# Gate one-hots of a PEER layer: where the row one-hots are written and how the column one-hots are divided

## What is computed

```python
def chunk(args):
    tc, ec, gc = args
    a = jnp.einsum('td,thkd->thk', tc, u_tab[ec])
    w = (gc * jax.nn.gelu(a)).astype(tc.dtype)
    return jnp.einsum('thk,thkd->td', w, v_tab[ec])
```

## Time and profile before

| | us |
|---|---|
| median of three runs | 2521.72 (2521.64 to 2522.34) |
| span of the profiled execution | 2525.9 |
| PE busy in it | 2230.9 (88%) |
| DVE busy | 1553.5 (62%) |
| ACT busy | 1185.2 (47%) |
| POOL busy | 1123.5 (44%) |
| first gate matmul of the first layer starts at | 792.92 |
| its last group of matmuls starts at | 903.67 |

### The profile page before, as it was taken

One profiled execution on the slowest core, in us unless ns is written; L12 is line 12 of the kernel. 1 busy time (PEld: TensorE's weight loads), 2 busy tenths in 40 slices (PEclk: granted clock), 3 DMA queues, 4 the chain that ended last, 5 costly groups with the idle time before them and its releaser, 6 DMA issues.

```text
span 2525.9 us, 46629 instructions
## 1 busy us (share of the span) xinstructions
PE 2230.9 (88%) x16556; PEld 2138.3 (85%) x16556; DVE 1553.5 (62%) x2319; ACT 1185.2 (47%) x2092; POOL 1123.5 (44%) x472
## 2 busy tenths in 40 slices
PE   5797789999997589999998967999999956999998
PEld 4686679999996588989997856899999955999998
DVE  7577348993004977888885952699800088555554
ACT  8522434555545743333433232455554476444443
POOL 0002036988886545555550301588988854000000
PEclk9798789999998999999998987999999999999999
DMA  7632144555553036556553312345555500555553
GB/s 264 216 115 78 45 141 134 183 179 187 183 181 102 0 116 218 206 209 224 208 215 120 125 34 92 125 151 190 181 180 181 182 17 0 175 182 182 183 183 108
DMA packets 103456, 378.58 MB, mean 150 GB/s; under 512 B 11489, under 2 KB 11873, under 8 KB 102881
## 3 DMA queue, kind: packets, MB, share of 16 engines
q1 hardware_dynamic: 102672, 373.74, 43.3%
q10 hardware_dynamic: 720, 4.00, 0.4%
HBM read 375.46 MB, written 2.23 MB: 150 GB/s over the span
## 4 chain that ended last, share of the span: by engine, by line
PE 34%; issue 24%; POOL 23%; DVE 12%; DMA 3%; ACT 2%; POOLq 1%; DVEq 1%; SPq 0%; ACTq 0%
POOL split_lo L471 19%; PE bank L1489 7%; PE bank L1490 7%; PE bank L1491 7%; PE bank L1556 3%; PE bank L1278 3%; POOL hots L482 2%; DVE w_lo L1170 2%; DMA ring<-stream 1%; DVE hots L1137 1%; PE bank L1241 1%; DVE split_lo L1169 1%; POOL ada_acc L498 1%; DMA ada_ring<-stream 1%; DVE hots L1135 1%
## 5 line engine op out<-in xcount | busy, mean ns | idle before, releaser
L471 POOL TENSOR_TENSOR split_lo<-ring,split_hi 128x1024 fp32r<-128x1024 f32 x296 | 729.3, 2489 | 246.6 <-ACT split_hi L688 246.3
L1489 PE MATMUL bank<-h_hi,split_hi 128*128 128x256 f32 x2304 | 657.0, 285 | 29.7 <-DVE h_lo L1079 21.3
L1490 PE MATMUL bank<-h_lo,split_hi 128*128 128x256 f32 x2304 | 654.4, 284 | 0.0
L1491 PE MATMUL bank<-h_hi,split_lo 128*128 128x256 f32 x2304 | 654.4, 284 | 0.0
L1489 PE MATMUL bank<-w_hi,split_hi 128*128 128x256 f32 x2048 | 589.4, 288 | 14.2 <-DVE w_lo L1170 14.2
L1490 PE MATMUL bank<-w_lo,split_hi 128*128 128x256 f32 x2048 | 586.8, 287 | 0.0
L1491 PE MATMUL bank<-w_hi,split_lo 128*128 128x256 f32 x2048 | 586.5, 286 | 0.0
L1169 DVE TENSOR_TENSOR split_lo<-ring,split_hi 128x1024 fp32r<-128x1024 f32 x248 | 375.3, 1513 | 251.6 <-ACT w_hi L764 251.6
L1489 PEld LDWEIGHTS bank<-h_hi,split_hi 128*128 128x128 f32 x2304 | 444.5, 193 | 34.7 <-issue 18.6
L763 ACT ACTIVATE split_hi<-ring 128x1024 fp32r<-128x1024 f32 x248 | 262.5, 1059 | 448.9 <-PE bank L1491 416.0
L1491 PEld LDWEIGHTS bank<-h_hi,split_lo 128*128 128x128 f32 x2304 | 444.8, 193 | 0.0
(11 more groups left out here) (267 smaller groups left out, 2776.9 us busy)
## 6 DMA issues: line engine op xcount, KB each, us to landing
ring<-stream SPq DMA_DIRECT2D x658, 512.0 KB, 3.3
ada_ring<-stream SPq DMA_DIRECT2D x48, 512.0 KB, 4.8
spill<-tables ACTq DMA_DIRECT2D x1, 1152.0 KB, 5.4
tables<-spill ACTq DMA_DIRECT2D x1, 1152.0 KB, 7.2
xT<-x_in SPq DMA_DIRECT2D x1, 1024.0 KB, 10.2
s5raw<-s5w ACTq DMA_DIRECT2D x2, 512.0 KB, 5.7
y_out<-hT SPq DMA_DIRECT2D x1, 1024.0 KB, 3.9
KM<-mixc SPq DMA_DIRECT2D x1, 576.0 KB, 8.3
```

The source lines that it names most:

```text
L471: gp.tensor_tensor(split_lo[:, j, :], ring[:, (e0 + j) % RING, :], split_hi[:, j, :].bitcast(F32), ALU.subtract)\
L1489: mm(dst, hi, x_hi, start=start, stop=False, skip_group_check=not group)
L1490: mm(dst, hi, x_lo, start=False, stop=False, skip_group_check=not group)
L1491: return mm(dst, lo, x_hi, start=False, stop=stop, skip_group_check=not group)
```

## The change

- POOL no longer multiplies a finished `hotA`. It writes it itself: for each token one `tensor_scalar` of 128x128 that compares `iota` with the token's column of `pick[:, 0]` and multiplies by its column of `pick[:, 2]`. That is 8 instructions a group in the place of one, 256 a layer, written out instead of in a loop. Before the first of a group it waits until PE has finished the group two before (`g_ready`), and for the first two groups until the gelus are done.
- DVE's line 1137 (rows, 128x1024) goes. Its line 1135 now writes the columns of 4 tokens (128x512) and raises `hot_eq`.
- ACT writes the columns of 4 tokens instead of 6: four Abs and a Relu of 128x512.
- PE waits for `hot_eq` as well, which stood behind `hot_ready` before.

```diff
+ACT_HOTS = 4
...
-                with pool.Fori(0, T // 16, 1) as i:
-                    for j in range(2):
-                        pool.wait_ge(hot_eq, i * 2 + (q0 + j + 1))
-                        gp.tensor_tensor(hotA[j], hotA[j], pick[:, 2, bass.ds(i * 16 + 8 * j, 8)].unsqueeze(2).broadcast_to([P, 8, P]),
-                                         ALU.mult).then_inc(hot_ready, 1)
+                pool.wait_ge(pick_ready, TT * (l + 1))
+                for n in range(T // 8):
+
+                    if n >= 2:
+                        pool.wait_ge(g_ready, T // 4 * l + 2 * n - 2)
+                    else:
+                        pool.wait_ge(gelu_done, KEYS // 2 * (l + 1))
+                    for t in range(8 * n, 8 * n + 8):
+                        last = gp.tensor_scalar(hotA[n % 2][:, t % 8, :], iota, pick[:, 0, t:t + 1], pick[:, 2, t:t + 1],
+                                                ALU.is_equal, ALU.mult)
+                    last.then_inc(hot_ready, 1)
...
-                    for t in range(2, 8):
+                    for t in range(8 - ACT_HOTS, 8):
...
-                    nc.scalar.activation(hotB[j][:, 2:8, :], hotB[j][:, 2:8, :], ACT.Relu, scale=-1.0, bias=1.0).then_inc(column_ready, 1)
+                    nc.scalar.activation(hotB[j][:, 8 - ACT_HOTS:8, :], hotB[j][:, 8 - ACT_HOTS:8, :], ACT.Relu, scale=-1.0, bias=1.0).then_inc(column_ready, 1)
...
-                    v.tensor_tensor(hotB[j][:, 0:2, :], iota.unsqueeze(1).broadcast_to([P, 2, P]),
-                                    pick[:, 1, bass.ds(n * 8, 2)].unsqueeze(2).broadcast_to([P, 2, P]), ALU.is_equal)
-                    v.tensor_tensor(hotA[j], iota.unsqueeze(1).broadcast_to([P, 8, P]),
-                                    pick[:, 0, bass.ds(n * 8, 8)].unsqueeze(2).broadcast_to([P, 8, P]), ALU.is_equal).then_inc(hot_eq, 1)
+                    m = 8 - ACT_HOTS
+                    v.tensor_tensor(hotB[j][:, 0:m, :], iota.unsqueeze(1).broadcast_to([P, m, P]),
+                                    pick[:, 1, bass.ds(n * 8, m)].unsqueeze(2).broadcast_to([P, m, P]), ALU.is_equal).then_inc(hot_eq, 1)
...
                     pe.wait_ge(hot_ready, i * 2 + (T // 8 * l + j // 2 + 1))
                     pe.wait_ge(column_ready, i * 2 + (T // 8 * l + j // 2 + 1))
+                    pe.wait_ge(hot_eq, i * 2 + (T // 8 * l + j // 2 + 1))
```

## The result

The changed kernel takes **2726.9 us** (median of 4 runs, 2722.3 to 2734.1) against 2522.0 for the kernel before in the same comparison. The ratio is 1.081, 95% interval 1.080 to 1.083: 205 us slower, where I had forecast 52. The direction held, the size did not, and the time lies above my range.

What follows compares the result with a forecast made beforehand. DVE and the buffer ring bound the gate stage at 3.50 us a group; POOL would become the bound at 3.92 + 0.46 = 4.38 us, adding 52.1 us over two layers: 2574 us, range 2470 to 2650.

Steps and rivals of the forecast that it cites:

- The ring: Gate stage's one-buffer loop: DVE columns, DVE rows, POOL, PE, last `weigh`; 6.99 us, two buffers in turn, 3.50 us a group.
- DVE's full 3.44 us: DVE's work per gate group, columns, rows and two `weigh`, read as about full within the 3.50 us a group takes.
- I take the start-up whole and 1.57 ns, the nearest row's: Price of POOL's new 128x128 gate instruction: 0.29 us start-up plus 128 x 1.57 ns, 0.49 us; eight take 3.92 us.
- rival 3: POOL's new instructions are heavier, column fetches costing extra: 0.65 us or more each, +134 us and more, above 2650; chance 0.09.
- upper bound of 0.81 us: Ceiling for POOL's new instruction: 0.55 us, what one single element takes in line 464, plus 127 x 2.06 ns.
- The shut-out: In the gate stage, POOL loses time to DVE's columns reading two SBUF operands: 0.46 us a group.
- POOL as the bound: In the changed gate stage POOL's period of 4.38 us a group sets the pace, against 3.50 before; PE needs 2.06.
- PE's new wait hidden: PE's wait for `hot_eq` before gate matmuls costs nothing as long as POOL needs over 2.3 us a group.
- the clock hidden but for the last burst: At PE's lower clock a burst takes about twice 2.06 us, under 4.38; last bursts cost 0 to 10 us, taken as 0.
- 512 t - 199 us: Predicted whole-kernel time difference, t being one new POOL instruction's time; zero at t = 0.39, 5.1 us for each 10 ns.
- no. 1 and 2: POOL's instruction cheaper: first, element rate halves, +1 us, chance 0.08; second, start-up mostly overlaps, -40 us, chance 0.28.
- No. 4: DVE's columns starve between POOL's instructions in the gate stage: period 5.4 us, +63 us on top, 2637 us; chance 0.03.

## Why the prediction was wrong in size

**What bounds the kernel before**: right. The ring and DVE's full 3.44 us stood as read; 0.26 us more on DVE alone cost 14 us.

**The cost of POOL's new instruction**: this is the step that failed, "I take the start-up whole and 1.57 ns, the nearest row's". It measured 0.787 us for 0.49. The start-up was 0.36 for 0.29, which is 512 x 0.07 = 36 us of the error. The time by element was 3.3 ns for 1.57, the other 116 us, and the runs say why: with an add in the place of the comparison the element takes 0.84 ns, with the comparison 2.5 ns more. With that add the instruction takes 0.447 us, the formula below gives +30 us, and the run was 32 above the kernel before. The row I had taken for the nearest was a multiplication. It was near in shape and not in operation. Both rivals that dealt with the element had it cheaper, not dearer. My rival 3 named the range in which the time fell ("above 2650", chance 0.09), with the columns as its cause; they cost 0.07 to 0.10 us, a third of the excess at most. My upper bound of 0.81 us did contain the value, at its very end, but I cut the range at 0.64.

**The shut-out**: 0.46 predicted, 0.42 to 0.44 measured.

**POOL as the bound, the division of the columns and PE's new wait hidden, the clock hidden but for the last burst**: all held. One sign that I had named misleads, though: "a gate stage over 150 us a layer with a lower PEclk would be the clock". Both came true (206 us from the first burst to the last, PEclk 0.54 to 0.58), and it is not the clock: a burst of 3.8 us fits into 6.6, and POOL was never idle.

**The sum**: 512 t - 199 us gives, with t = 0.787, +204 us. Measured were +205. So the mechanism and the arithmetic stood, and one term, the price of the instruction, carried the error of 152 us. That the two agree within 1 us is in part luck. In the first layer the steps were 6.64 us and not 8 x 0.787 + 0.46 = 6.76, 3.5 us less in 31; POOL began 1.4 us later than I had put it; the last burst, put at nothing, cost 1.6. And the measurement does not carry that agreement: the four executions of the changed kernel spread over 12 us, and the profiled ones of the two kernels lie 197 us apart.

**The rivals**: no. 1 and 2 needed an instruction of 0.39 us or less; even with an add for the comparison it is 0.447. No. 4 did not happen: DVE's columns took 0.68 us and did not wait.

## What to carry to other kernels

When one operation replaces another on GpSimd, take the price from a row with the same kind of operation, not only the same shape: here a compare-and-multiply costs four times an add-and-multiply for each element (3.3 and 0.84 ns). If there is no such row, the upper bound belongs into the range in full. And before an engine with slack is given eight instructions for one, multiply the difference through: at 512 instructions each 10 ns were 5 us.

## What the runs showed of the hardware

- GpSimd `tensor_scalar` f32, two operations: add and mult 0.34 us + 0.84 ns by element (0.447 at 128, 1.198 at 1024); is_equal and mult 0.36 us + 3.3 ns (0.787 and 3.78). One is_equal at 128: 0.60 us. Two columns for two constants: 0.07 us by the spacing of undisturbed instructions.
- GpSimd `tensor_tensor` f32 with one operand repeated: 0.18 us + 1.68 ns by element (0.395 at 128, 1.897 at 1024).
- VectorE `tensor_scalar` is_equal and mult of 128x128: one every 0.29 us, so for this form VectorE is 2.7 times as fast as GpSimd.
- With PE idle for 2.9 us before each burst of matmuls, the granted clock was at 0.5 to 0.6 through the stage, and a burst took 3.8 instead of 2.06 us; with gaps of 1.44 us in the kernel before it was 1.00.
